# A three-layer block on one core: layer 1's convolution taken first, its taps spread between the norms, four weight halves beside the attention

## The reference, cut to what matters

```
h = rms_norm(x, norm_g)
c_a, c_b, c_g, d_q, d_kv, d_bg, d_g, m_q, m_g = split_cols(h @ w_in, ODD_SPLITS)
y_c = conformer_conv(c_a, c_b, ...) * silu(c_g)      # 31 taps over time, 512 channels, then rms_norm, silu
y_d = nsa(d_q, d_kv, sigmoid(d_bg), ...) * silu(d_g)  # 8 heads x (compressed, selected, windowed) attention
y_m = memory_attention(m_q, mem_n, m_wkv, ...) * silu(m_g)   # 4 heads over 256 memory tokens
x = x + concat([y_c, y_d, y_m]) @ w_out
```

## Time and profile before

| what | us |
|---|---|
| median of 3 runs | 1029.19 (1028.76 to 1029.42) |
| the profiled execution, its own time | 1031.47 |
| its span, first to last instruction | 1029.7 |
| mean granted TensorE clock, as a share of 2.4 GHz | 0.961 |
| TensorE busy | 946.3 (92%) |
| VectorE busy | 445.9 (43%) |
| ScalarE busy | 328.3 (32%) |
| GpSimd busy | 440.5 (43%) |

### The profile page before, as it was taken

One profiled execution on the slowest core, in us unless ns is written; L12 is line 12 of the kernel. 1 busy time (PEld: TensorE's weight loads), 2 busy tenths in 40 slices (PEclk: granted clock), 3 DMA queues, 4 the chain that ended last, 5 costly groups with the idle time before them and its releaser, 6 DMA issues.

```text
span 1029.7 us, 14942 instructions
## 1 busy us (share of the span) xinstructions
PE 946.3 (92%) x5860; PEld 849.2 (82%) x5860; DVE 445.9 (43%) x948; ACT 328.3 (32%) x607; POOL 440.5 (43%) x561
## 2 busy tenths in 40 slices
PE   4999899999999897989898999889999898999995
PEld 4888788888888775768798998789898898998994
DVE  1453555511357799661498126701020434322133
ACT  2201343102000144331344475444020443443441
POOL 0040000100110100002399678898270398999992
PEclk9999989999999988889899999989999999999999
DMA  8443223243434400141164435353534155555551
GB/s 340 135 163 123 82 82 102 67 159 123 162 124 164 164 6 37 41 169 50 44 246 142 143 123 187 111 173 102 204 124 164 42 179 167 177 194 181 177 181 55
DMA packets 37637, 139.33 MB, mean 135 GB/s; under 512 B 4288, under 2 KB 4288, under 8 KB 37312
## 3 DMA queue, kind: packets, MB, share of 16 engines
q1 hardware_dynamic: 37424, 136.97, 39.0%
q10 hardware_dynamic: 144, 1.41, 0.3%
HBM read 137.32 MB, written 1.05 MB: 134 GB/s over the span
## 4 chain that ended last, share of the span: by engine, by line
PE 24%; POOL 22%; DVE 2%; ACT 1%; issue 1%; DVEq 0%; ACTq 0%; POOLq 0%
POOL w_lo L1993 22%; PE psum L488 7%; PE psum L489 6%; PE psum L490 5%; PE psum L491 5%; DVE y_lo L1378 1%; PE psum L552 1%; PE psum L543 0%; POOL rstd L2001 0%; ACT w_hi L1003 0%; DVE h_rows L1446 0%; DVE h_lo L1352 0%; DVE h_rows L1974 0%; ACT act_tmp L1064 0%; ACT h_hi L1029 0%
## 5 line engine op out<-in xcount | busy, mean ns | idle before, releaser
L1993 POOL TENSOR_TENSOR w_lo<-raw,w_hi 128x256 fp32r<-128x256 f32 x536 | 405.5, 798 | 127.9 <-ACT w_hi L1003 65.7
L488 PE MATMUL psum<-w_whole,h_whole 128*128 128x256 f32 (+1 forms) x960 | 227.8, 393 | 3.0 <-ACT h_whole L1041 2.2
L2001 POOL TENSOR_TENSOR rstd<-mean_sq,minus_half 128x2 f32<-128x2 f32 (+4 forms) x20 | 34.6, 1731 | 456.4 <-DVE mean_sq L1390 456.4
L489 PE MATMUL psum<-h_hi,w_hi 128*128 128x256 f32 x704 | 202.6, 288 | 12.6 <-POOL w_lo L1993 12.2
L488 PEld LDWEIGHTS psum<-w_whole,h_whole 128*128 128x128 f32 x960 | 183.4, 198 | 28.9 <-ACT h_whole L1041 2.6
L490 PE MATMUL psum<-h_lo,w_hi 128*128 128x256 f32 x704 | 201.1, 286 | 0.0
L491 PE MATMUL psum<-h_hi,w_lo 128*128 128x256 f32 x704 | 200.9, 285 | 0.0
L1003 ACT ACTIVATE w_hi<-raw 128x1024 fp32r<-128x1024 f32 x136 | 139.5, 1055 | 118.6 <-DMA raw<-in_blocks 78.5
L489 PEld LDWEIGHTS psum<-h_hi,w_hi 128*128 128x128 f32 x704 | 137.1, 195 | 14.8 <-issue 14.6
L490 PEld LDWEIGHTS psum<-h_lo,w_hi 128*128 128x128 f32 x704 | 137.1, 195 | 0.1
L491 PEld LDWEIGHTS psum<-h_hi,w_lo 128*128 128x128 f32 x704 | 137.1, 195 | 0.0
(11 more groups left out here) (268 smaller groups left out, 1307.6 us busy)
## 6 DMA issues: line engine op xcount, KB each, us to landing
raw<-in_blocks SPq DMA_DIRECT2D x136, 512.0 KB, 3.5
w_whole<-in_blocks SPq DMA_DIRECT2D x96, 512.0 KB, 4.3
w_late<-in_blocks SPq DMA_DIRECT2D x20, 512.0 KB, 4.4
early<-in_early SPq DMA_DIRECT2D x1, 1647.0 KB, 7.2
attention<-in_late ACTq DMA_DIRECT2D x1, 1380.0 KB, 7.8
rows<-in_mem SPq DMA_DIRECT2D x2, 512.0 KB, 3.5
x<-in_x SPq DMA_DIRECT2D x1, 1024.0 KB, 9.4
out_x<-h_rows SPq DMA_DIRECT2D x2, 512.0 KB, 2.6
```

The source lines that it names most:

```text
L488: return nc.tensor.matmul(out, lhs[0], rhs[0], start=start, stop=stop, skip_group_check=shared_bank)
L489: nc.tensor.matmul(out, lhs[0], rhs[0], start=start, stop=False, skip_group_check=shared_bank)
L1993: ins = nc.gpsimd.tensor_tensor(lo[:, at], full[:, at], hi[:, at].bitcast(F32), ALU.subtract)
L2001: rstd_ready.mark(nc.gpsimd.tensor_tensor(rstd[:, n % 2, 0:width], mean_sq[:, n % 2, 0:width], minus_half[:, 0:width], ALU.pow), name, pool)
```

## The change

Line numbers after the change are 1 to 2 higher in the first half of the file, up to 5 higher in VectorE's helpers.

- TensorE projects `c_b` half 0, `c_a` half 0, `c_b` half 1, `c_a` half 1 first of all in layer 1 (`CONV_IN`), then `d_q`, `dkv1`, `m_qg1`; `cmp_w1` follows. `dkv2` now is what covers the waits behind `cmp_w1`, and is finished ahead of the attention.
- `c_g` and `d_g` stand entirely in the attention's filler: 4 halves, 32 steps over 28 units.
- The taps stand behind the halves of the convolution (14 and 12 pairs), in the norms (3 in `dq`, 2 in `dk`, 3 in `mq1`, 4 in `kc`), and behind `dq` (4), `dk` (6) and the memory gate (4). 10 pairs are left for units 0 to 4.
- `CONV_END` is 5 and `TURN_AT` is units 6 and 9, so that the whole end of the convolution stands 12 units earlier, where the same kinds of units stand.
- The copies out of PSUM of `mk1`, `dq` and `dk` move from VectorE to ACT. The convolution's input is placed elsewhere in `rows`. The memory keys are normalized first.

The diff, cut to its core:

```diff
-FILL = [both_of(L0_FILL), [("c_g", 1), ("d_g", 0), ("d_g", 1)]]
+FILL = [both_of(L0_FILL), both_of(["c_g", "d_g"])]
...
-CONV_END = 17
-TURN_AT = {18: 0, 21: 1}
+CONV_END = 5
+TURN_AT = {6: 0, 9: 1}
+BESIDE_NORM = {"dq": 3, "dk": 2, "mq1": 3, "kc": 4}
+CONV_IN = [(n, half) for half in range(2) for n in ("c_b", "c_a")]
...
(TensorE, layer 1)
             turned(pe, "x1_2", "x1_3")
+            for name, half in CONV_IN:
+                for _ in features_piece(name, half, h_whole):
+                    pass
+            normed.wait(pe, "mk1")
+            turn_pair("mk1", ...)
             project("d_q", h_whole)
             project("dkv1", h_whole)
...
-            project_features("c_b", h_whole)
-            normed.wait(pe, "mk1")
-            turn_pair("mk1", ...)
+            project("m_qg1", h_whole)
             normed.wait(pe, "dk")
...
-            project_features("c_a", h_whole)
-            project("dkv2", h_whole, (HC, 24))
-            project("m_qg1", h_whole)
...
-            beside = (s for half in range(2) for s in rows_piece("c_g", half, h_whole))
+            beside = chain(rows_piece("dkv2", 0, h_whole), rows_piece("dkv2", 1, h_whole, 24))
+            next(beside)
             next(beside)
             normed.wait(pe, "mq1")
...
-            for _ in range(KT + 2 - 3):
-                next(beside)
+            for _ in beside:
+                pass
             normed.wait(pe, "kc")
...
(VectorE)
-                if name in ("mq1", "kc"):
-                    taps(4)
+                if name in BESIDE_NORM:
+                    taps(BESIDE_NORM[name])
...
             odd_sources("x1_", h_whole[0], E("l1_norm"))
             memory_keys(1)
-            for half in range(2):
+            for half, n in ((0, 14), (1, 12)):
                 settle(proj, ("c_b", half))
                 arrive(proj, ("c_a", half))
...
-                taps(6)
+                taps(n)
```

85 lines of the change are left out of this document (41 added, 44 removed).

## The result

The changed kernel takes 1003.81 us (median of 4 runs, 1001.88 to 1006.10), the kernel before 1028.97 us beside it (4 runs, 1028.27 to 1029.42): a ratio of 0.9754, 95% interval 0.9717 to 0.9792. It is faster by 25.2 us, where 15.7 were forecast, and lies under the low end of the range (1007). The profiled execution took 1001.88 us, with a span of 1000.1 us.

What follows compares the result with a forecast made beforehand. TensorE's work was taken to bound layer 1's front, and VectorE, about half of it taps, the attention's units 5 to 15. Terms -9.6 + 3.0 + 1.6 - 10.7 = -15.7 us gave 1013.5 us, range 1007 to 1024.

Steps and rivals of the forecast that it cites:

- The front: Layer 1 from 251 us to the first scores: 10.95 us removed, 1.35 added, -9.6 us, attention starting at 346.8.
- Two added waits: In the front: 0.9 us behind ACT's later `dk` copies, and 0.45 us for the gates' copy before VectorE's last small products.
- The clock loss: Low clock behind the 24-column projection: 1.78 us leaves the front, 1.3 us comes back in units 0 to 5.
- The near ties of VectorE's offer: In the front, four places where VectorE's results come about when TensorE needs them, with no lateness claimed.
- rival C: VectorE late in the front because POOL's powers wait for the taps beside them: +4 us, 1017.5 us; chance 0.12.
- Units 0 to 5: Start of the attention: 4 more filler steps, two of them free, and the low clock behind the 24 columns; +3.0 us.
- Units 5 to 15: Attention units taking the convolution's end, modelled on units 17 to 27 before, with 11 filler steps: 39.2 us, +1.6 us.
- Units 15 to 27: Attention units free of taps and convolution, at layer 0's pace plus one low-clock stretch: 31.1 us, -10.7 us.
- Rival B: Low clock stays in the free attention units, 3.39 us each, 40.7 instead of 31.1 us: 1023 us; chance 0.20.
- A: The forecast itself for the whole kernel: 1013.5 us, 1007 to 1019 with the middle units' and clock's bounds; chance 0.58.
- Rival D: TensorE bounds the whole attention at a low clock, which takes 120 us: +14.4 us, 1043.6 us; chance 0.06.
- rival E: Work only moves: the ten filler steps come back in full and free units stay as long; about 1029 us; chance 0.04.

Runs made afterwards that it cites:

- half_in_front: Changed kernel with the first half of `c_g` (8 filler steps) projected ahead of the attention, 24 steps left beside it; 1012.86 us, ratio 0.9845 to the kernel before.
- split_norm: Changed kernel with the convolution's norm on VectorE cut in two, its product and gains moved to unit 12; 1006.44 us, ratio 0.9770 to the kernel before.
- two_swaps: Changed kernel with `kc_t` copied ahead of the gates' products and `dk` copied ahead of the memory gate's tanh; 1004.07 us, ratio 0.9748 to the kernel before.
- filler_first: Changed kernel with all 32 filler steps in units 0 to 13 and none in units 14 to 27; 1014.20 us, ratio 0.9844 to the kernel before.
- idle_products: `filler_first` with two unread 256-column products added at each loop step from 15 to 27; 1011.74 us, ratio 0.9828 to the kernel before.
- late_wait: Changed kernel with four added VectorE passes over 1024 unread elements ahead of unit 21; 1012.17 us, ratio 0.9825 to the kernel before.
- narrow_first: Changed kernel with `dkv2`'s 24-column half projected before its 256-column half; 1014.24 us, ratio 0.9846 to the kernel before.

## Why the prediction was right in direction and short in size

**The front: right.** Forecast -9.6, measured -9.80. The first scores stand at 344.73; with the 1.85 us by which this trace starts the front sooner that is 346.6, where 346.8 was forecast. Two added waits were named, 0.9 and 0.45 us net; the rows show 1.40 ahead of `cmp_w1` and 1.64 ahead of the first scores, where 1.12 stood before: 0.5 and 0.1 more than said. The clock loss left the front, as said, and came back at the start of the attention. That the 24 columns carry it is not shown, since in `half_in_front` they bring none. Kernel after, columns as in the first view:

```profile
344.00:346.00 2.00, 1.27 (x6) 1.18 (x8) 0.19 (x1) 0.00 (x0) 0.00 (x0) 0.50 0.79 264
...
348.00:350.00 2.00, 2.00 (x6) 1.55 (x6) 1.93 (x5) 0.71 (x4) 0.00 (x0) 0.50 0.01 4
```

The near ties of VectorE's offer held: TensorE waits for neither `mq1` nor the small products behind `cmp_w1`, nor for `kc`. POOL's powers in the kernel after, in order of time:

```profile
294.93 3.13 POOL L2001 TENSOR_TENSOR rstd<-mean_sq,minus_half 128x16 f32<-128x16 f32 x1 [42.44 <-DVE mean_sq L1395]
309.90 1.87 POOL L2001 TENSOR_TENSOR rstd<-mean_sq,minus_half 128x8 f32<-128x8 f32 x1 [11.84 <-DVE mean_sq L1395]
323.78 1.87 POOL L2001 TENSOR_TENSOR rstd<-mean_sq,minus_half 128x8 f32<-128x8 f32 x1 [12.00 <-DVE mean_sq L1395]
```

With taps beside them they are longer by 0.23 us each than alone (2.90 and 1.64), for 16 columns as for 8. This is what the sum had; rival C, a power that waits for whole taps, did not occur. The rule of the Trainium skill, "SBUF — State Buffer", section "Who interferes with whom", that such instructions block each other, would be seen here as 0.23 us and no more.

**Units 0 to 5: right.** +2.79 for +3.0: TensorE's work went up by 3.3 us, the clock took 1.4 more, and the 1.95 us wait is gone.

**Units 5 to 15: the step that failed first.** The forecast took units 17 to 27 of before as the model, "36.86 us", added the work of three filler steps, and let the model's clock come along with it, 0.72. The model's long piece was right: the wait of unit 12 is 2.54 us behind the same norm. The stretch's split shows what wasn't: in the model idle 5.7, clock 8.7, work 22.4 us; after the change idle 5.0, clock 2.9, work 25.8. The term that was mis-sized is the clock's, by 5.8 us, and the forecast's miss in these units is 5.4. In the model the clock fell twice, for some 10 us each time, behind waits of 1.88 and 3.42 us. Kernel before:

```profile
420.00:432.00 12.00, 12.00 (x58) 9.98 (x59) 5.40 (x21) 3.82 (x15) 0.00 (x0) 0.57 0.01 1
441.00:452.00 11.00, 9.74 (x38) 7.74 (x38) 8.67 (x26) 6.48 (x21) 0.00 (x0) 0.53 0.01 2
```

In the kernel after it fell once, behind the 2.54 us, from 388 to 395 us:

```profile
388.00:392.00 4.00, 4.00 (x16) 2.83 (x17) 2.52 (x9) 2.94 (x7) 0.00 (x0) 0.52 0.24 96
```

What made the difference is the filler that the forecast counted as work alone: with the model's 8 steps these units run at the model's 0.72 and take 40.42 us (`half_in_front`), with 11 at 0.90 and take 33.70. The forecast had 39.2. (`half_in_front` is 3.6 us over the model at the same clock and filler; it is idle for 8.3 us where the model was for 5.7.) That the three steps act by shorter waits and by a shorter low clock, both, is what the split says; their shares are as rough as it is.

The bound of -4 for "the model's low clock rises" was written down, and it is nearly what came (-3.84). It was treated as an end of the range and not as the likely case.

**Units 15 to 27: the same error from the other side.** Rival B (the low clock stays, 3.39 us a unit) was wrong, and A was right in kind, but 31.1 us were forecast for 27.73. Of the 3.4 us, 1.6 are the low stretch that I put in beside the full-clock pace and that didn't come, and 1.8 are the unit's price: 1.52 us from layer 0, where it is (27.73 - 13 x 0.863) / 12 = 1.38 here. A third of layer 1's units are compressed ones, whose turn is 0.38 us where the others' is 0.49; that is 0.4 of the 1.8 us, and the rest isn't traced.

**The sum.** The two failed steps are 5.44 + 3.34 = 8.8 us of the 9.2 by which the sum was short; 0.4 are from the steps that held. Some 7 of the 8.8 are one mistake, the clock: 5.4 where it was carried over from a stretch with less filler, and 1.6 where a low stretch was put in that didn't come. The range's low end, 1007, held the clock's bound of the middle units, but not together with a gain in the last ones; both hang on the same cause, so their errors add up: -3.84 and -14.04 with the rest as forecast give 1005.

**Small slips in the prediction.** Rival B gives units 17 to 27 "a third" of layer 0's filler per unit; 8 steps in 10 units against 39 in 12 is a quarter. Rival D's 64.6 us come out at 64.5, and rival E's ten steps at 8.6 us, not 9.6. None of them moves the forecast. The 0.2 us "with a semaphore" in the front's added wait is a guess that no row gives; the wait came out at 1.40 where 0.9 was said.

**What stays open.** What length of wait takes the clock down isn't a single number here. A wait of 1.58 us at unit 6 left it up in the kernel after, one of 1.52 took it down in `split_norm` and 2.09 did in `two_swaps`. What TensorE did before the wait may matter too, and no run separates that; nor do the runs say why the 24-column products went with a low clock in three kernels and not in `half_in_front`, or why the clock came back at 425 us in `filler_first`. Nor is it known why the kernel before's second block ran at 0.83 at 499.6 to 520 us in its profiled execution.

## What to carry to other kernels

Where TensorE's clock falls behind its own waits, count a wait of some 2 us at about twice its length and more where little filler follows (13 us at 0.51 behind 3.42 us in `half_in_front`), and take the clock of a changed stretch from the waits and the filler that it will have, not from the stretch that served as a model. Independent wide products set between small ones can be free: before you move filler out of a stretch of small matmuls, split that stretch into idle, clock and work, and see whether the filler is what holds the clock. And a front that gets shorter may pay nothing if the next place where another engine is late is then reached sooner; look for it first, and move both.

## What the runs showed of the chip

- TensorE can be busy without a gap and still be granted only 0.50 of its clock for 15 us (`filler_first`, 410 to 425 us), when it does transposes, scores and 64-column products. The Trainium skill, "TensorE: Matmul & The Clock Gate", Part 1, has the gate follow how busy TensorE has been; the busy share of the records doesn't show it, since it is 5.00 of 5.00 us in `filler_first` at 0.50 and in `idle_products` at 1.00.
- With two products of 256 columns more in each of those units the clock was 1.00 from 415 us on, and units 15 to 27 took 27.86 us where they took 27.43 without (`idle_products`).
- The same ten units with 8 filler steps ran at 0.72 and took 40.42 us, with 11 at 0.90 and took 33.70 (`half_in_front`, changed kernel).
- A VectorE piece that made TensorE wait 2.10 us cost 4.16 us up to unit 27 (`late_wait`).
- Moving 24-column products ahead of 256-column ones, among small products, with the same work, cost 8 to 10 us (`narrow_first`: 0.50 at 340 to 345 us with TensorE busy 5.00 of 5.00).
